# Block products by Strassen's scheme in the second feed-forward layer of a two-block transformer kernel

## Chip, cores and metric

One Trainium2 chip (trn2), one core. The metric is the device time of one execution in microseconds; three executions of the kernel before took 2068.88, 2069.16 and 2074.09 us, median 2069.16.

## What is computed

All in float32, 256 tokens, width 1024. A first transformer block (attention of two kinds, 32 experts with 4 chosen per token) is followed by two blocks: one with retention and one with an S5 state-space mixer, each with a gated, convolved feed-forward layer. The change concerns the feed-forward layer of the last block alone:

```python
def conv_ffn(h, w_up, conv_w, conv_b, w_down):
    val, gate = jnp.split(h @ w_up, 2, axis=-1)          # 1024 -> 2 x 2816
    gate = lax.conv_general_dilated(gate, conv_w, ..., padding=[(CONV_W - 1, 0)], ...) + conv_b   # 3 taps over tokens
    return (jax.nn.silu(gate) * val) @ w_down            # 2816 -> 1024

x = x + g2 * conv_ffn(h, ffn_w_up[i], ffn_conv_w[i], ffn_conv_b[i], ffn_w_down[i])
return rms_norm_2(x) * final_norm_g
```

## The kernel before

Activations lie transposed: a feature tile is 128 partitions, 256 tokens are the columns. Weights come through `ring`, six slots of 2 MB ("slabs"), filled by SP's queue in a fixed order; a slot is loaded again when the product that reads it has ended (`slab_left`). `plan()` (L221) numbers every PSUM chunk in the order in which PE makes them, and deals them to four banks in turn; `places()` (L353) deals the slabs to slots. Each engine's program is written out by hand. `begin` waits until a bank's last chunk was read, `end` signals `acc_ready`, readers wait for it with `read_ready` and give the bank back with `read_done`; `copied` waits for that signal. Four slots are held by the S5 mixer (`HELD`) and given back at slab `("glu", 2)`.

**Up.** 11 slabs of 8 k tiles x 512 features. `features` (L1058, matmul at L1074) makes 4 output tiles of 8 matmuls, each 128x128 weights on 256 columns; two output tiles make a chunk, a "pair". Pairs 0 to 10 are values: ACT copies them to `val` (`copy`, L1902). Pairs 11 to 21 are gates: ACT writes the tap of lag 0 and the bias (L2140), VectorE adds the lags 1 and 2 straight from PSUM (L2896, four operations), ACT takes tanh (L2157), and `finish` (L2918) makes the product with the value pair in two VectorE operations (L2923, L2926), one pair later.

**Down.** 8 slabs of 22 k tiles x 128 features; each is one chunk of 22 matmuls on 256 columns (L1074 again). Those of slab 0 wait pair by pair for `act_ready`. `add_to_x` (L2434) adds each to x, times the gate g2.

Ahead of up stands a norm: L2234 to L2263 on VectorE, then scale and shift of eight tiles on ACT (L1862), for each of which PE's first matmuls wait. Behind down stands the last norm: squares on ACT (L1808), sums on PE (L1096), L2232 to L2263 on VectorE, and the stores. GpSimd works for the S5 mixer (L3085 to L3204) and has nothing to do in this layer.

Other lines that are read below: L1394 and L1460 (gather and turning in the experts), L1745 and L1775 (S5 and glu products), L3018 (glu), L2837 and L2838 (retention, from PSUM), L3098 to L3109, L3185 and L3189 (GpSimd, for S5). GpSimd's L3098 to L3103 ran beside VectorE's `finish` of the first of the two feed-forward layers, which uses the same lines.

## Time and profile before

| | |
|---|---|
| median of three executions | 2069.16 us |
| span of the profiled execution | 2066.0 us (its time as a whole is not given; the median is 3.2 us above the span) |
| PE busy | 1958.7 us, 95% |
| VectorE busy | 632.7 us, 31% |
| ScalarE busy | 392.6 us, 19% |
| GpSimd busy | 201.1 us, 10% |
| second feed-forward layer, first up to last down matmul | 1827.11 to 2055.63 us |

Names in the rows: PE is TensorE's matmul, PEld its weight load, DVE is VectorE, ACT is ScalarE, POOL is GpSimd, SP the engine that issues the loads. Times are us from the start of the span, durations us unless marked ns. Each float32 matmul of the program stands as two records. "arena", "consts", "smalls", "ring" and "tiny" are SBUF tensors. Idle time of an engine that nobody waits for costs nothing.

### The profile page before, as it was taken

To read this page: it belongs to the slowest core of one execution; us is meant where nothing else is said; L and a number is where in the kernel's file an instruction comes from. 1 tells how busy PE (TensorE), PEld (TensorE's weight loads), DVE (VectorE), ACT (ScalarE), POOL (GpSimd) and SP (SyncE) were. 2 spreads that over 40 slices of the span, in tenths; PEclk is the share of its full clock that TensorE was granted. 3 is DMA by queue.
4 is the path that set the end of the run, shared out by engine and by line. 5 is a ranking of instruction groups with operands and counts; after the bars stand their busy time and mean duration, and the time that the engine had idled before them with its cause. 6 is when DMAs were issued, how large, how long until landed. Compare 5 with 4: busy or idle time off the path is not lost.

```text
span 2066.0 us, 24454 instructions
## 1 busy us (share of the span) xinstructions
PE 1958.7 (95%) x9820; PEld 1233.4 (60%) x9820; DVE 632.7 (31%) x1401; ACT 392.6 (19%) x759; POOL 201.1 (10%) x274
## 2 busy tenths in 40 slices
PE   7999999999898999989899999999999999999998
PEld 5645654433333443333334375788888889888887
DVE  3767342213212222112122255331004216210421
ACT  3125211110111111101111021220113215320211
POOL 0000000000000000000000000010745932200000
PEclk9999999999999999999999999999999999999999
DMA  9987799999999999999999996834343342634330
GB/s 373 367 306 247 272 378 407 427 425 426 429 428 429 429 428 429 428 429 428 429 428 428 414 365 221 319 112 145 121 163 123 140 166 95 237 135 146 112 112 21
DMA packets 120080, 615.40 MB, mean 298 GB/s; under 512 B 5344, under 2 KB 9568, under 8 KB 90560
## 3 DMA queue, kind: packets, MB, share of 16 engines
q1 hardware_dynamic: 118240, 604.43, 73.2%
q0 software_dynamic: 1760, 9.83, 1.3%
q8 instruction: 59, 0.97, 0.2%
q14 instruction: 21, 0.17, 0.0%
HBM read 613.20 MB, written 1.05 MB: 297 GB/s over the span
## 4 chain that ended last, share of the span: by engine, by line
PE 71%; DMA 20%; DVE 5%; ACT 2%; issue 1%; SPq 1%; POOL 1%; DVEq 0%; ACTq 0%; POOLq 0%
PE psum L1074 32%; PE psum L1439 20%; DMA ring<-in_w_in_dram 17%; PE psum L1085 3%; PE psum L1394 2%; PE psum L1405 2%; DMA arena<-in_cT_dram 2%; PE psum L1316 1%; PE psum L1589 1%; PE psum L1189 1%; DMA ring<-in_w_out_dram 1%; PE psum L1775 1%; PE psum L1121 1%; PE psum L1460 1%; PE psum L1217 1%
## 5 line engine op out<-in xcount | busy, mean ns | idle before, releaser
L1439 PE MATMUL psum<-ring,arena 128*64 128x512 f32 (+1 forms) x3200 | 687.4, 603 | 63.8 <-DMA ring<-in_w_in_dram 62.4
L1074 PE MATMUL psum<-arena,ring 128*128 128x256 f32 (+1 forms) x3072 | 680.4, 384 | 2.2 <-ACT arena L1862 1.4
L1074 PEld LDWEIGHTS psum<-arena,ring 128*128 128x128 f32 x3072 | 581.7, 190 | 99.0 <-issue 18.8
L1439 PEld LDWEIGHTS psum<-ring,arena 128*64 128x64 f32 (+1 forms) x3200 | 222.2, 135 | 502.7 <-issue 432.2
L1995 ACT ACTIVATE arena<-psum 128x512 f32<-128x512 f32 (+1 forms) x144 | 79.1, 571 | 730.5 <-PE psum L1439 724.9
L2575 DVE TENSOR_SCALAR arena<-consts,arena 128x64 f32<-128x64 f32 (+2 forms) x64 | 15.7, 309 | 317.3 <-PE psum L1439 317.3
L2896 DVE SCALAR_TENSOR_TENSOR consts<-psum,smalls,consts 128x255 f32<-128x255 f32 (+1 forms) x88 | 38.4, 478 | 229.9 <-ACT consts L2140 229.1
L2600 DVE TENSOR_TENSOR arena<-psum,arena 128x512 f32<-128x512 f32 x60 | 38.5, 683 | 221.6 <-PE psum L1460 221.6
L2557 DVE SCALAR_TENSOR_TENSOR x<-psum,mod,x 128x256 f32<-128x256 f32 x128 | 55.6, 479 | 136.0 <-PE psum L1405 135.9
L3068 POOL DMA_DIRECT2D arena<-in_pos_dram x1 | 0.5, 541 | 907.4 <-PE psum L1568 907.4
L1405 PE MATMUL psum<-arena 128*128 128x256 f32 (+1 forms) x272 | 68.1, 392 | 3.6 <-issue 1.5
L1902 ACT ACTIVATE arena<-psum 128x512 f32<-128x512 f32 (+1 forms) x49 | 27.3, 558 | 224.6 <-PE psum L1074 173.4
L1405 PEld LDWEIGHTS psum<-arena 128*128 128x128 f32 (+1 forms) x272 | 47.5, 189 | 30.8 <-issue 14.9
L2434 DVE SCALAR_TENSOR_TENSOR x<-psum,mod,x 128x256 f32<-128x256 f32 x28 | 13.0, 482 | 162.9 <-PE psum L1074 152.3
L1394 PE MATMUL psum<-arena 128*128 128x128 f32 x512 | 61.5, 280 | 0.0
L1394 PEld LDWEIGHTS psum<-arena 128*128 128x128 f32 x512 | 60.1, 196 | 0.0
L1085 PE MATMUL psum<-ring,arena 128*128 128x512 f32 x128 | 55.1, 592 | 0.0
L1808 ACT ACTIVATE sq<-x 128x512 f32<-128x512 f32 x24 | 15.0, 629 | 206.4 <-DVE x L2434 180.7
L2286 DVE SCALAR_TENSOR_TENSOR arena<-ring,cond,arena 128x512 f32<-128x512 f32 x70 | 52.6, 752 | 2.5
L2140 ACT ACTIVATE consts<-psum,smalls 128x256 f32<-128x256 f32 x44 | 22.5, 562 | 116.0 <-PE psum L1074 116.0
L1460 PE MATMUL psum<-consts,arena 128*128 128x128 f32 x256 | 37.8, 281 | 6.7 <-DVE arena L2600 5.6
L1460 PEld LDWEIGHTS psum<-consts,arena 128*128 128x128 f32 x256 | 27.1, 140 | 26.6 <-issue 19.3
(397 smaller groups left out, 1657.2 us busy)
## 6 DMA issues: line engine op xcount, KB each, us to landing
ring<-in_w_in_dram SPq DMA_DIRECT2D x120, 2048.0 KB, 17.1
ring<-in_w_out_dram SPq DMA_DIRECT2D x60, 2048.0 KB, 17.2
ring<-in_w_ada_dram SPq DMA_DIRECT2D x36, 2048.0 KB, 13.7
ring<-in_w_up_dram SPq DMA_DIRECT2D x22, 2048.0 KB, 7.9
ring<-in_w_ret_dram SPq DMA_DIRECT2D x12, 2048.0 KB, 16.4
ring<-in_w_down_dram SPq DMA_DIRECT2D x16, 1408.0 KB, 5.9
ring<-in_w_qkv_dram SPq DMA_DIRECT2D x4, 2048.0 KB, 20.1
ring<-in_w_in_dram SPq DMA_DIRECT2D x8, 1024.0 KB, 17.6
```

Source lines behind the costliest of these rows:

```text
L1074: ins = nc.tensor.matmul(bank(c)[:, at:at + n], w[:, k, m * P:m * P + P], r, start=(k == 0), stop=(k == k_tiles - 1))
L1085: ins = nc.tensor.matmul(bank((key, first_chunk + t))[:, 0:width], lhs(k, t), w[:, k, at:at + width], start=(k == 0), stop=(k == KD - 1))
L1394: ins = nc.tensor.matmul(psum[:, c, m * P:m * P + width], h_tok[:, t, k * P:k * P + P], sel[:, t, 0:width], start=(t == 0), stop=(t == TT ...
L1405: ins = nc.tensor.matmul(psum[:, 6 + c % 2, m * T:m * T + T], y[:, k * P:k * P + P], g, start=True, stop=True)
L1439: ins = nc.tensor.matmul(psum[at:at + size, p, :], act[:, k, n:n + size], w, start=(k < 3 - halves), stop=(k >= KD - 3 + halves))
L1460: ins = nc.tensor.transpose(out, of, con("ident"))
L1902: read_done(nc.scalar.activation(out, src, ACT.Copy, scale=scale), key)
L1995: nc.scalar.activation(out, src, ACT.Copy).then_inc(signal, 1)
L2286: ins = V.scalar_tensor_tensor(out=out, in0=w[:, k, :], scalar=c[:, k, :], in1=out, op0=ALU.mult, op1=ALU.add)
L2557: ins = V.scalar_tensor_tensor(out=x[:, k, :], in0=psum[:, 6 + c % 2, m * T:m * T + T], scalar=mod[:, 40 + k, 0:1], in1=x[:, k, :], op0=AL ...
L2600: ins = V.tensor_tensor(dst.rearrange("p k (e n) -> p k e n", n=CAP), src.rearrange("p k (e n) -> p k e n", n=CAP), bb.unsqueeze(3).to_bro ...
L2896: ins = V.scalar_tensor_tensor(out=cv[:, a, lag:T], in0=ps[:, a, 0:T - lag], scalar=w[:, 2 - lag, k:k + 1], in1=cv[:, a, lag:T], op0=ALU.m ...
```

## The change

The up product of layer 1 is cut per slab into a 2 x 2 block form: output features in two halves of 256 (i), k tiles in two halves of 4 (j), tokens in two halves of 128 (l). The down product is cut per two slabs: i is the slab, j the parity of the k tile, l the token half. Seven block products (Winograd's form) take the place of eight. PE makes them on 128 columns each: 7 x 8 matmuls per up unit, 7 x 11 per down unit.

- GpSimd makes S1 to S4 of the weights, four chained operations per unit, S1 in place of A21, the others in two sets of room taken from the arena and from two ring slots, so the ring has four slots in this layer. In down, S4 takes the room of S2, after product 6.
- VectorE makes T1 to T4 of the tokens: for up once, before it; for down four subtractions of 128x128 at the end of each pair.
- ACT copies product 1; VectorE adds up the others in seven operations per unit. Value and gate then both lie in SBUF, and the lagged sums read the gate from there. A pair is ready later: the blocks of i = 1 after products 5 and 4, those of i = 0 after products 2 and 3.
- The first down unit makes products 1, 6, 7, 5 jointly, pair by pair in the order in which the pairs become ready, then 2, 4, 3. Each down unit adds four 128x128 blocks to x; ACT's squares wait for `down_added`.
- The first up unit takes the order 1, 5, 6, 7, 2, 4, 3, and product 1 waits for four h tiles.

The core of the diff (of the functions, `seven_products` is PE's, the first `seven_up` ACT's, those from `with_sixth_product` on VectorE's, `weight_sums` and what follows it GpSimd's):

```diff
+PRODUCTS = {1: ("A11", "B11"), 2: ("A12", "B21"), 3: ("S4", "B22"), 4: ("A22", "T4"), 5: ("S1", "T1"),
+            6: ("S2", "T2"), 7: ("S3", "T3")}
+SEVEN = (1, 6, 7, 5, 2, 4, 3)
+SEVEN_FIRST = (1, 5, 6, 7, 2, 4, 3)
+SUM_NUMBER = {"S3": 1, "S1": 2, "S2": 3, "S4": 4}
+GATE_PAIRS = {layer: [0] + [m for s in range(6, 11) for m in (2 * s - 10, 2 * s - 11)] for layer in SEVEN_UP}
...
         if key == ("glu", 2):
-            queue = held + queue
+            queue = held[:2] + queue
...
+            def seven_products(key, a, b, blocks_ready=None, together=()):
...
+                def starts(p):
+                    begin((key, p))
+                    if PRODUCTS[p][0] in SUM_NUMBER:
+                        pe.wait_ge(weights_summed, 4 * unit + SUM_NUMBER[PRODUCTS[p][0]])
...
+                if together:
+                    for p in order[:4]:
+                        starts(p)
+                    for k in together:
+                        blocks_ready(k)
+                        for p in order[:4]:
+                            ins = part(p, k, 0, together[0], together[-1])
...
+                for p in order[4:] if together else order:
+                    starts(p)
+                    if blocks_ready and not together:
+                        blocks_ready(PRODUCTS[p][1])
+                    for m in range(m_tiles):
+                        for k in range(n_k):
+                            ins = part(p, k, m, 0, n_k - 1)
+                    end(ins)
...
+            def seven_up(layer):
+                done = 0
+                for s in range(11):
+                    late = range(done, done + pairs_of(s - 1))
+                    done += len(late)
+                    for n in late[:1]:
+                        if n:
+                            tanh(layer, n - 1)
+                        conv_begin(layer, n)
+                    copy_first(("up", layer, s), 2)
+                    for n in late[1:]:
+                        tanh(layer, n - 1)
+                        conv_begin(layer, n)
...
+            def with_sixth_product(key, m_tiles):
+                copied(dve, (key, 1))
+                read_done(plus_product(key, 6, m_tiles, first_product, with_sixth), (key, 6))
+                copied(dve, (key, 6))
+            def with_seventh_and_fifth(key, m_tiles, out):
+                read_done(plus_product(key, 7, m_tiles, with_sixth, with_seventh), (key, 7))
+                own.mark(plus_product(key, 5, m_tiles, with_sixth, with_fifth))
+                copied(dve, (key, 7))
+                read_done(plus_product(key, 5, m_tiles, with_seventh, out), (key, 5))
+                dve.wait_ge(dve_step, own.n)
+            def lagged_sums(layer, n):
...
+                for lag in (1, 2):
+                    for a in range(2):
+                        k = 2 * m + a
+                        own.mark(V.scalar_tensor_tensor(out=cv[:, a, lag:T], in0=gate[:, a, 0:T - lag],
+                                                        scalar=w[:, 2 - lag, k:k + 1], in1=cv[:, a, lag:T],
+                                                        op0=ALU.mult, op1=ALU.add))
+                    dve.wait_ge(dve_step, own.n)
+                V.memset(tiny[:, 499:500], 0.0).then_inc(conv_ready, 1)
+            def finish_pair(layer, n):
...
+                own.link(V.scalar_tensor_tensor(out=t, in0=t, scalar=1.0, in1=cv, op0=ALU.add, op1=ALU.mult))
...
+                V.scalar_tensor_tensor(out=v, in0=t, scalar=0.5, in1=v, op0=ALU.mult, op1=ALU.mult
+                                       ).then_inc(act_ready, 1)
+                dve.wait_ge(act_ready, 11 * layer + n + 1)
...
+                own.mark(sub("T3", "B22", "B12"))
+                own.link(sub("T1", "B12", "B11"))
+                own.link(sub("T2", "B22", "T1"))
+                sub("T4", "B21", "T2").then_inc(tokens_summed, 1)
+            def seven_up(layer):
+                first_sums(layer)
+                done = 0
+                for s in range(11):
+                    key = ("up", layer, s)
+                    late = range(done, done + pairs_of(s - 1))
+                    done += len(late)
+                    for n in late[:1]:
+                        lagged_sums(layer, n)
+                    with_sixth_product(key, 2)
+                    for n in late[:1]:
+                        if n:
+                            finish_pair(layer, n - 1)
+                    with_seventh_and_fifth(key, 2, up_out(s, 1, 1))
+                    for n in late[1:]:
+                        lagged_sums(layer, n)
+                    read_done(plus_product(key, 2, 2, first_product, up_out(s, 0, 0)), (key, 2))
+                    read_done(plus_product(key, 4, 2, with_seventh, up_out(s, 1, 0)), (key, 4))
+                    for n in late[1:]:
+                        finish_pair(layer, n - 1)
+                    read_done(plus_product(key, 3, 2, with_fifth, up_out(s, 0, 1)), (key, 3))
+                for n in range(done, 11):
+                    lagged_sums(layer, n)
+                    finish_pair(layer, n - 1)
+                finish_pair(layer, 10)
...
+            def weight_sums(key, a, free=None):
...
+                add("S3", "A11", "A21", ALU.subtract).then_inc(weights_summed, 1)
+                pool.wait_ge(weights_summed, n + 1)
+                add("S1", "A21", "A22", ALU.add).then_inc(weights_summed, 1)
+                pool.wait_ge(weights_summed, n + 2)
+                add("S2", "S1", "A11", ALU.subtract).then_inc(weights_summed, 1)
+                pool.wait_ge(weights_summed, n + 3)
+                if free:
+                    read_ready(pool, free)
+                add("S4", "A12", "S2", ALU.subtract).then_inc(weights_summed, 1)
...
+            read_ready(pool, ("s5y", S5_PARTS - 1))
+            for s in range(11):
+                in_place(("up", 1, s))
+                if s >= 2:
+                    read_ready(pool, (("up", 1, s - 2), 3))
+                weight_sums(("up", 1, s), up_weights(1, s))
+            for s in range(0, 8, 2):
+                for n in range(2):
+                    in_place(("down", 1, s + n))
+                read_ready(pool, (("down", 1, s - 4) if s >= 4 else ("up", 1, 8 + s // 2), 3))
+                weight_sums(("down", 1, s), down_weights(1, s), (("down", 1, s), 6))
```

`pairs_of(s)` is the number of gate pairs that up unit s makes: 0 to unit 4, one in unit 5, then two. `GATE_PAIRS` gives their order. So in unit s the engines work on the gate pairs of unit s - 1.

## Rows read from the trace of the kernel before

**Rows 1.** The page: VectorE's busy share, PE's and the granted clock in 40 slices.

```profile
PE 1958.7 (95%) x9820; PEld 1233.4 (60%) x9820; DVE 632.7 (31%) x1401; ACT 392.6 (19%) x759; POOL 201.1 (10%) x274
...
PEclk9999999999999999999999999999999999999999
```

**Rows 2.** Chain in order of time (start, us, what): the layer.

```profile
1827.11 228.53 PE psum L1074 x1056
```

**Rows 3.** Timeline (start, us, engine, line, xcount, idle before): gates of the layer.

```profile
1932.47 1.78 DVE L2896 SCALAR_TENSOR_TENSOR consts<-psum,smalls,consts 128x255 f32<-128x255 f32 x4 [3.57 <-ACT consts L2140]
...
1934.40 0.69 DVE L2923 SCALAR_TENSOR_TENSOR consts<-consts 128x512 f32<-128x512 f32 x1
1935.12 0.69 DVE L2926 SCALAR_TENSOR_TENSOR arena<-consts,arena 128x512 f32<-128x512 f32 x1
...
1938.25 1.02 ACT L2140 ACTIVATE consts<-psum,smalls 128x256 f32<-128x256 f32 x2 [5.37 <-PE psum L1074]
...
1939.38 1.79 DVE L2896 SCALAR_TENSOR_TENSOR consts<-psum,smalls,consts 128x255 f32<-128x255 f32 x4 [3.56 <-ACT consts L2140]
```

**Rows 4.** Timeline of VectorE in down: two of the eight additions to x.

```profile
1998.68 0.48 DVE L2434 SCALAR_TENSOR_TENSOR x<-psum,mod,x 128x256 f32<-128x256 f32 x1 [8.93 <-PE psum L1074]
2008.18 0.48 DVE L2434 SCALAR_TENSOR_TENSOR x<-psum,mod,x 128x256 f32<-128x256 f32 x1 [9.01 <-PE psum L1074]
```

**Rows 5.** Timeline of PE in the experts: matmuls on 128 columns.

```profile
263.44 5.45 PE L1394 MATMUL psum<-arena 128*128 128x128 f32 x32
...
303.11 1.09 PE L1460 MATMUL psum<-consts,arena 128*128 128x128 f32 x8
...
305.70 3.74 PE L1394 MATMUL psum<-arena 128*128 128x128 f32 x32
309.27 0.38 PE L1485 MATMUL psum<-consts,arena 128*128 128x128 f32 x2
```

**Rows 6.** Timeline of ACT and PE at the start of up.

```profile
1826.36 4.04 ACT L1862 ACTIVATE arena<-arena,mod,aff 128x256 f32<-128x256 f32 x8 [2.20 <-DVE arena L2263]
...
1827.11 3.07 PE L1074 MATMUL psum<-arena,ring 128*128 128x256 f32 x12 [0.45 <-ACT arena L1862]
```

**Rows 7.** Groups of GpSimd by form (busy us, mean ns): 512 and 1024 elements.

```profile
L3101 POOL TENSOR_TENSOR consts<-arena,tiny 128x512 f32<-128x512 f32 x4 | 4.2, 1057 | 0.0
...
L3185 POOL TENSOR_TENSOR consts<-tiny 128x1024 f32<-128x1024 f32 x1 | 1.9, 1912 | 0.1
```

**Rows 8.** DMA issues (KB each, median us to landing), 1780 to 2066.

```profile
ring<-in_w_down_dram SPq DMA_DIRECT2D x8, 1408.0 KB, 6.0
```

**Rows 9.** Timeline of VectorE: operations from PSUM on 256 and 128 columns, and one in glu.

```profile
1368.94 0.42 DVE L2837 TENSOR_TENSOR sq<-psum,consts 128x256 f32<-128x256 f32 x1
1369.28 0.28 DVE L2838 TENSOR_TENSOR sq<-psum,consts 128x128 f32<-128x128 f32 x1
...
1812.84 0.69 DVE L3018 SCALAR_TENSOR_TENSOR arena<-arena 128x512 f32<-128x512 f32 x1 [5.30 <-ACT arena L2214]
```

**Rows 10.** Timeline of VectorE and GpSimd where both run.

```profile
1588.52 1.78 DVE L2896 SCALAR_TENSOR_TENSOR consts<-psum,smalls,consts 128x255 f32<-128x255 f32 x4 [2.04 <-ACT consts L2140]
1588.49 1.09 POOL L3102 TENSOR_TENSOR arena<-arena,consts 128x512 f32<-128x512 f32 x1
...
1597.32 1.06 POOL L3098 TENSOR_TENSOR arena<-arena,tiny 128x512 f32<-128x512 f32 x1
1597.35 1.58 DVE L2923 SCALAR_TENSOR_TENSOR consts<-consts 128x512 f32<-128x512 f32 x1
1598.34 1.51 POOL L3099 TENSOR_TENSOR consts<-arena,tiny 128x512 f32<-128x512 f32 x1
1598.96 1.43 DVE L2926 SCALAR_TENSOR_TENSOR arena<-consts,arena 128x512 f32<-128x512 f32 x1
...
1693.56 1.88 POOL L3189 COPY sq<-tiny 128x2016 f32<-128x2016 f32 x1
1694.37 1.34 DVE L2234 TENSOR_TENSOR rstd<-rstd 128x256 f32<-128x256 f32 x1
```

**Rows 11.** Windows of PE (stretch, its length, busy, granted clock, DMA share, GB/s).

```profile
263.00:266.00 3.00, 3.00 (x20) 0.65 1.05 442
```

More of the change, by code:

```diff
@@ L221, in plan @@
 def plan():
-    chunks, slabs, bank, use = {}, {}, {}, {}
+    chunks, slabs, bank, use, units = {}, {}, {}, {}, {}
     uses = [0] * 6
@@ L243, in slab, with seven @@
         slabs[key] = len(chunks)
+    def seven(keys, order=SEVEN):
+        units[keys[0]] = len(units), order
+        chunk(*((keys[0], p) for p in order))
+        for key in keys:
+            slabs[key] = len(chunks)
     chunk(("norm", 1))
@@ L316, in ffn @@
         for s in range(11):
-            slab(("up", layer, s), 2)
+            if layer in SEVEN_UP:
+                seven([("up", layer, s)], SEVEN if s else SEVEN_FIRST)
+            else:
+                slab(("up", layer, s), 2)
             if layer == 0 and s == 0:
                 chunk(("cols", 8))
-        for s in range(8):
-            slab(("down", layer, s), 1)
+        for s in range(0, 8, 2):
+            if layer in SEVEN_DOWN:
+                seven([("down", layer, s), ("down", layer, s + 1)])
+            else:
+                slab(("down", layer, s), 1)
+                slab(("down", layer, s + 1), 1)
     ffn(0)
@@ L336, in plan @@
     chunk(("norm", 8))
-    return chunks, bank, use, slabs, rope_uses, before_loop
-CHUNK, BANK_OF, USE, SLABS, ROPE_USES, SLABS_1 = plan()
+    return chunks, bank, use, slabs, rope_uses, before_loop, units
+CHUNK, BANK_OF, USE, SLABS, ROPE_USES, SLABS_1, UNITS = plan()
 SLAB_KEYS = list(SLABS)
+UNIT_KEYS = list(UNITS)
 EARLY_SLABS = 1
@@ L812, in copied, with product, summed_tokens @@
             eng.wait_ge(acc_free[BANK_OF[key]], USE[key] + 1)
+        def product(key, p, m_tiles):
+            return psum[:, BANK_OF[(key, p)], 0:P * m_tiles]
+        def summed_tokens(kind, layer, n):
+            before = sum(4 * (at in SEVEN_UP) + 11 * (at in SEVEN_DOWN) for at in range(layer))
+            return before + n + (4 if kind == "down" else 0)
         def ln_of(guess):
@@ L874, in transformer_blocks_kernel @@
             7: [[(("glu", 2 + s // 2), s % 2)] for s in range(4)],
-            8: [[(("down", 1, 2 * s + a), 0) for a in range(2)] for s in range(4)],
         }
@@ L2118, in ffn @@
                 apply(5 + 2 * layer)
+                if layer in SEVEN_UP:
+                    seven_up(layer)
+                    for s in range(0, 8, 2):
+                        copy_first(("down", layer, s), 1)
+                    return
                 if layer == 0:
@@ new lines, in plus_product @@
+            def plus_product(key, p, m_tiles, a, out):
+                read_ready(dve, (key, p))
+                a, src = a[:, 0:P * m_tiles], product(key, p, m_tiles)
+                if len(out.shape) == 3:
+                    a, src = two(a), two(src)
+                else:
+                    out = out[:, 0:P * m_tiles]
+                return V.tensor_tensor(out, src, a, ALU.add)
+            def with_sixth_product(key, m_tiles):
+                copied(dve, (key, 1))
+                read_done(plus_product(key, 6, m_tiles, first_product, with_sixth), (key, 6))
+                copied(dve, (key, 6))
```

166 lines of the change are left out of this document (added).

## The prediction

> **What bounds the kernel now.** I read the page first: PE is busy nearly throughout at full granted clock and DVE under a third of the span [rows 1]. The chain in order of time then shows the second feed-forward layer as one piece, 228.53 us of L1074 with no other engine in it [rows 2]. So only matmul time counts there. One gate pair takes 6.91 us from L2896 to L2896 [rows 3], so an up slab (two pairs) takes 13.82 us; a down slab takes 9.50 us [rows 4]. The trace holds two records for each float32 matmul of the program: 1056 records are 11 x 32 + 8 x 22 = 528 matmuls, 0.433 us each, that is 0.216 us for half the columns. The span is 2066.0 us and the page gives no other time of that execution; the median of the runs is 3.2 us above the span. I add the change to the median.
>
> **Fewer columns: a gain.** A block product multiplies by 128 columns instead of 256. Per up unit 7 x 8 = 56 such matmuls stand for 32 full ones, per down unit (two slabs) 77 for 44. Their price: 32 records of L1394 run from 305.70 to 309.27 [rows 5], 0.1116 us each, so 0.223 us a matmul. Bounds: half a full one, 0.216, and the eight records of L1460, (1.09 - 0.28) / 7 = 0.116 us each, so 0.231 [rows 5]. I take 0.2235: same form, and the longest run. Up unit 12.52 us, 1.30 less, 11 times: -14.3. Down unit 17.21 against 19.0, 4 times: -7.2. **Clean gain 21.5 us.** A product takes 1.79 us in up, 2.46 in down. The two price bounds move about 700 matmuls (those that PE itself paces) by -5 to +5 us.
>
> **Start of up.** Before, PE starts at 1827.11, after the first h tile, and loses 0.5 us to tiles arriving each 0.49 us [rows 6]. Now product 1 waits for four tiles, 1.3 us later; T1 (0.69 us, one 128x512 operation, as L2923) and T2 fall under products 1 and 5. Net +0.8.
>
> **GpSimd's sums** are four chained TENSOR_TENSOR per unit of 1024 elements, 1.91 us each [rows 7], in down of 1408, 2.6 us by the slope from 512 to 1024. That is 7.7 us against a unit of 12.52 and 10.4 against 17.21, begun a whole unit ahead: hidden from PE. The ring has four slots instead of six; a down slab lands in 6.0 us [rows 8] and is asked for two units ahead: hidden. One place is short: S4 of the first down unit waits for product 6 and holds up the next unit's three sums: 10.7 us after product 6, wanted at about 10.4. +0.3. Up slabs 0 and 1 are now loaded when the first two glu slabs are done, and GpSimd's sums for them meet VectorE's glu operations, which sit idle 5.30 us ahead of each [rows 9]: hidden, and over before the norm. The queue of SP gets no new wait that PE notices.
>
> **VectorE's own work**, per gate unit. Seven reads of a product (0.42 us each, L2837 [rows 9]; back to back 0.36, chained 0.46): 2.8. Two lagged sums, 1.93 each from L2896 to L2923 [rows 3]: 3.86. Two finishes, 1.45 each, now with four subtractions of 128x128 (L2838 0.28 [rows 9], chained 0.32, together 1.14): 5.18. Sum 11.84 us in 12.52: just hidden. ACT, in its order tanh, conv_begin, copy of product 1, needs 4.1 us (1.02 for a pair [rows 3]) and its waits are met half a unit ahead. In the first six units VectorE has only the 2.8; in a down unit seven reads and four additions of 0.28 to 0.32, some 3.5 us in 17.2: hidden. Behind each read in VectorE's queue stand the lagged sums and finishes, and behind the reads stands PE, since four banks let it run at most four products ahead: a late VectorE stops PE within one unit.
>
> **The last pair.** After product 3 of unit 10 VectorE still owes the read, then lagged 9, finish 8, lagged 10, finish 9, finish 10: 1.93 + 2.59 + 1.93 + 2.59 + 2.59 = 11.6 us. PE covers 8.9 us with the ten earlier pairs of the joined products (40 matmuls). VectorE is 1.7 us late there, so even undisturbed PE waits 4.5 us. Before it waited for none.
>
> **The disturbance on which the sign hangs.** While GpSimd runs a TENSOR_TENSOR, VectorE operations with both inputs in SBUF wait for it: L2923 and L2926, 0.69 us alone, take 1.58 and 1.43 at 1597.35 while L3098 and L3099 run, and L3099 takes 1.51 instead of 1.06 [rows 10]. They take turns, and one GpSimd operation costs VectorE its length less 0.3 us. It holds for long ones: L2234 (0.42 alone) waits 0.92 us, until the 1.88 us L3189 has 0.15 us left [rows 10]. Operations that read PSUM are not held: the four L2896 at 1588.52 take 1.78 us, as without GpSimd [rows 3, 10]. In the change the lagged sums read the gate from SBUF, so they and the finishes and subtractions are all held; only the seven reads are free. Holding time per gate unit is 7.7 us of GpSimd plus some 8.5 us of VectorE, 16 us against 12.52. So I work out the chain, with 1.6 us for a held operation of 1024 and 2.3 for one of 1408. Time 0 is PE's end of unit 6, when the sums for unit 8 begin.
> Unit 7: read of product 3, 0.45; lagged sum held four times, 1.93 + 6.3 (8.7); read of 6 (9.1); finish (11.7); read of 7 at 12.1, which frees the bank for product 3, so PE ends unit 7 at 13.9, not 12.5. From there the sums for unit 9 hold a lagged operation 1.45, a finish 0.75 (0.8 goes under two reads), then 1.6 twice: 5.4. The read of 7 in unit 8 is at 12.1 + 11.84 + 5.4 = 29.3. In unit 9: again 5.4, and 7.0 by the first three sums of down, which GpSimd starts as soon as slab down 1 lands: 53.5. In unit 10 GpSimd waits: 65.4. Then 6.5 to the end of the unit's reads and 11.6 for the pairs: 83.5. Undisturbed PE would want the last pair at 4 x 12.52 + 8.9 = 59.0. **VectorE makes it 24.6 us late** (24 us of holding, of 15 operations and 30.7 us; 4.5 had come without it, but VectorE's slack of 0.7 a unit and its lateness are used up in it).
>
> The Trainium skill states the same coupling and speaks against this change: "SBUF — State Buffer", section "Who interferes with whom" and the list before it, calls the shared port pair an exclusive lock held for the whole instruction, against a VectorE operation with two SBUF inputs. The rows agree in kind and are 0.3 us short of the whole; by the whole length the sum would be some 4 us higher. The rest stands without it.
>
> **Clock.** With waits of up to 3.7 us in each gate unit and short bursts before the last pair, PE may resume at half clock: at 263 the granted clock is 0.65 and L1394 takes 5.45 us instead of 3.74 [rows 5, 11]. It matters once, after the last pair: +1.7 (0 to 3.4).
>
> **Tail.** Behind the last matmul one more 128x128 operation and two waits: +0.3.
>
> **Sum:** -21.5 + 0.8 + 0.3 + 24.6 + 1.7 + 0.3 = +6.2, so 2075.
>
> **Forecast and rivals.** A measurement of this kernel can tell 0.3%, 6.2 us, from no change.
> Forecast, 0.5: the gain is eaten in units 7 to 10, +6, slower by a hair. Its own range, with holding between 18 and 28 us: -1 to +12.
> Rival 1, 0.25, faster: the holding is mostly hidden, since GpSimd's operations fall on VectorE's reads and idle time (it has both in every unit, 2.8 and 0.7 us), or are shorter beside each other than here. It decides if less than about 10 of the 24 us is left. With none: -21.5 + 0.8 + 4.5 + 0.3 + 0.3 = -15.6, so 2054; half kept gives -8. For it: the steady unit fits without holding. Against: rows 10, where each meeting is paid.
> Rival 2, 0.15, clearly slower: PE falls to half clock in each gate unit, where a stall of 3.7 us precedes three products that the reads wait for; then the clock delays VectorE too. At 1.7 us in each of units 7 to 10 and twice after: 8.5 more in place of 1.7, +13; with each GpSimd operation paid whole +17, 2086. Against: the clock is 1.0 through the span's other waits [rows 1].
> Rival 3, 0.1: the half-width matmuls gain less, 0.231 us, and holding is as forecast: +5 more, 2080. That seven products stand for eight is certain from the counts.
>
> **Numbers.** 2075. Low: 2056, taking in most of rival 1; high 2086, rivals 2 and 3. The likeliest case's own range is 2068 to 2081. Faster by over 0.3%: 0.27 (rival 1 and a sliver). Within: 0.33 (the lower half of the forecast, part of rival 1). Slower: 0.40.
>
> **What would show it.** PE spacing 0.112 us a record in units 0 to 6, and 12.5 us a unit; DVE L2923 and the subtractions at 1.5 to 2.3 us instead of 0.69 and 0.28 in units 7 to 9, reads unchanged; PE waiting on DVE some 25 us between unit 7 and the first down product 2; POOL busy some 126 us more (11 x 7.7 + 4 x 10.4). The forecast is wrong if the lagged sums keep 0.48 us under a running GpSimd operation, or if the gate units last 12.5 us.

## The result, and the profile after the change

The kernel with the change is slower: 2088.8 us (median of 4 runs, 2086.78 to 2090.35) against 2071.6 us for the kernel before on the same chip (4 runs, 2068.88 to 2075.22). The ratio is 1.0087, 95% interval 1.0070 to 1.0103; the medians are 17 us apart. The forecast was 2075 in a range of 2056 to 2086: the side was right, the size was not, and the result lies outside the range.

The first part of the page after the change answers to [rows 1]:

```profile
PE 1954.6 (94%) x10612; PEld 1252.6 (60%) x10612; DVE 758.2 (36%) x1565; ACT 392.6 (19%) x763; POOL 357.7 (17%) x334
...
PEclk9999999999999999999999999999999999999899
```

PE is busy 4.1 us less in a span that is 22.5 us longer (2088.5 against 2066.0). DVE gained 125.5 us of busy time, though the change gives it far less arithmetic than that, and POOL gained 157, where 126 had been foreseen.

In the text below, "the layer" is the time from the first up matmul to the end of the last down matmul: 228.53 us before [rows 2]. After the change the chain of work in order of time reads (start, us, what; pieces in between are left out):

```profile
1831.12 75.29 PE psum L1179 x672
...
1906.86 4.82 DVE consts L3135 x2
...
1923.16 4.83 DVE consts L3135 x2
...
1967.99 5.55 DVE consts L3135 x2
1973.57 6.53 DVE consts L3135 x2
...
2013.58 6.32 POOL ring L3559 x2
...
2026.51 16.62 PE psum L1179 x132
2043.51 7.82 DMA ring<-in_w_down_dram
...
2062.91 14.99 PE psum L1179 x132
```

The layer now lasts from 1831.12 to 2077.90, **246.8 us**, 18.3 more. The one piece of [rows 2] has broken up. Units 0 to 5 are still PE's alone, 672 records in 75.29 us. From 1906, the first gate unit, the chain runs through VectorE's lagged sums, and in down through GpSimd's sums and a load. The other 4.2 us of the two spans: PE's first up matmul stands 2.22 us behind ACT's first h tile (0.75 in [rows 6]), the tail is 0.25 us longer, and 2.5 us came before the layer, where the code is the same; I leave those out.

VectorE's timeline after the change (start, us, engine, line, form, xcount). L3135 are the lagged sums, L3146, L3150 and L3158 a finish with its subtractions:

```profile
1923.08 9.87 DVE L3135 SCALAR_TENSOR_TENSOR consts<-ring,smalls,consts 128x255 f32<-128x255 f32 x4
...
1937.03 1.78 DVE L3135 SCALAR_TENSOR_TENSOR consts<-ring,smalls,consts 128x255 f32<-128x255 f32 x4
...
1939.52 2.09 DVE L3146 SCALAR_TENSOR_TENSOR consts<-consts 128x512 f32<-128x512 f32 x1
1941.65 2.72 DVE L3150 SCALAR_TENSOR_TENSOR arena<-consts,arena 128x512 f32<-128x512 f32 x1
1944.40 5.19 DVE L3158 TENSOR_TENSOR arena<-arena 128x128 f32<-128x128 f32 x4
...
1960.16 7.50 DVE L3158 TENSOR_TENSOR arena<-arena 128x128 f32<-128x128 f32 x4
...
1967.92 12.18 DVE L3135 SCALAR_TENSOR_TENSOR consts<-ring,smalls,consts 128x255 f32<-128x255 f32 x4
```

and GpSimd's beside it:

```profile
1922.85 2.36 POOL L3559 TENSOR_TENSOR arena<-ring 128x1024 f32<-128x1024 f32 x1 [6.49 <-PE psum L1179]
1925.29 2.41 POOL L3559 TENSOR_TENSOR ring<-ring 128x1024 f32<-128x1024 f32 x1
...
1938.71 10.41 POOL L3559 TENSOR_TENSOR ring<-ring 128x1024 f32<-128x1024 f32 x4 [6.04 <-PE psum L1179]
...
1969.90 9.92 POOL L3559 TENSOR_TENSOR ring<-ring 128x1408 f32<-128x1408 f32 x3
2013.55 12.81 POOL L3559 TENSOR_TENSOR ring<-ring 128x1408 f32<-128x1408 f32 x4 [33.73 <-PE psum L1179]
```

Four lagged sums take 1.78 us where GpSimd is idle (1937.03), as in [rows 3], and 9.87 us beside four of GpSimd's sums (1923.08): one VectorE operation for each of GpSimd's, held 2.02 us each. At 1967.92 GpSimd works on 1408 elements and the four take 12.18. The kind of holding is that of [rows 10]; the length is new: a sum of 1024 elements takes 2.40 us and one of 1408 3.18. The groups by form (busy us, mean ns) say the same, and that the reads of PSUM (L3109) are not held:

```profile
L3559 POOL TENSOR_TENSOR ring<-ring 128x1408 f32<-128x1408 f32 x16 | 50.9, 3184 | 48.2 <-PE psum L1179 45.8 <-issue 1.8
L3559 POOL TENSOR_TENSOR ring<-ring 128x1024 f32<-128x1024 f32 x21 | 50.4, 2398 | 16.0 <-PE psum L1179 14.6
...
L3109 DVE TENSOR_TENSOR consts<-psum,consts 128x256 f32<-128x256 f32 x33 | 13.5, 424 | 32.6 <-PE psum L1179 32.5
```

PE's timeline shows where it stood (the bracket is its wait):

```profile
1949.98 3.78 PE L1179 MATMUL psum<-sq,ring 128*128 128x128 f32 x16 [6.06 <-DVE ring L3109]
...
1980.70 3.78 PE L1179 MATMUL psum<-sq,ring 128*128 128x128 f32 x16 [7.18 <-DVE consts L3109]
...
2026.51 51.37 PE L1179 MATMUL psum<-arena,ring 128*128 128x128 f32 x440 [2.81 <-POOL ring L3559]
```

The two products behind the long waits take 3.78 us where 16 records otherwise take 1.79, at half clock (granted 0.50 from 1949.9 to 1953.5). The last line hides 2.2 us more: 440 records at 0.1117 are 49.2 us, not 51.37. Most of it is half clock too, behind the wait of 2.81 us. PE's windows (stretch, its length, PE busy, granted clock, DMA share, GB/s):

```profile
2026.50:2028.00 1.50, 1.49 (x11) 0.81 1.02 436
2028.00:2030.00 2.00, 2.00 (x11) 0.50 0.78 332
```

The first 132 of these records take 16.62 us (in the chain above), against 14.90 in a later version that does not wait there. So in down GpSimd's sums cost 2.8 us of waiting once, 1.7 of half clock behind it and some 0.5 over the rest, 5.0 in all.

### The profile page after: what moved, and what is told of

Read it like the earlier page. It is cut to its first block, busy times and chain, and to the rows that moved or that the text cites. A ratio compares the mean times of both kernels' runs of the same rounds, so it can differ in the third digit from the quotient of the medians.

```text
span 2088.5 us, 26401 instructions
## 1 busy us (share of the span) xinstructions
PE 1954.6 (94%) x10612; PEld 1252.6 (60%) x10612; DVE 758.2 (36%) x1565; ACT 392.6 (19%) x763; POOL 357.7 (17%) x334
## 3 DMA queue, kind: packets, MB, share of 16 engines
q8 instruction: 65, 1.06, 0.2%
## 4 chain that ended last, share of the span: by engine, by line
PE 66%; DMA 20%; DVE 8%; ACT 2%; POOL 2%; issue 2%; SPq 1%; DVEq 0%; ACTq 0%; POOLq 0%
PE psum L1160 21%; PE psum L1560 20%; DMA ring<-in_w_in_dram 18%; PE psum L1179 7%; PE psum L1206 3%; PE psum L1515 2%; DVE consts L3135 2%; PE psum L1526 2%; DMA ring<-in_w_qkv_dram 1%; PE psum L1437 1%; PE psum L1710 1%; PE psum L1310 1%; PE psum L1929 1%; POOL ring L3559 1%; PE psum L1242 1%
## 5 line engine op out<-in xcount | busy, mean ns | idle before, releaser
L1160 PE MATMUL psum<-arena,ring 128*128 128x256 f32 (+1 forms) x2016 | 453.6, 387 | 1.8 <-ACT arena L2018 0.9
L1160 PEld LDWEIGHTS psum<-arena,ring 128*128 128x128 f32 x2016 | 382.9, 191 | 70.6 <-issue 18.0
L2151 ACT ACTIVATE arena<-psum 128x512 f32<-128x512 f32 (+1 forms) x144 | 79.1, 571 | 730.2 <-PE psum L1560 724.6
L1179 PE MATMUL psum<-arena,ring 128*128 128x128 f32 x1048 | 126.9, 282 | 9.3 <-POOL ring L3559 2.8
L1179 PEld LDWEIGHTS psum<-arena,ring 128*128 128x128 f32 x1048 | 124.3, 199 | 10.7 <-issue 7.6
L3559 POOL TENSOR_TENSOR ring<-ring 128x1024 f32<-128x1024 f32 (+1 forms) x42 | 113.9, 2714 | 64.4 <-PE psum L1179 60.4
L2761 DVE SCALAR_TENSOR_TENSOR x<-psum,mod,x 128x256 f32<-128x256 f32 x128 | 55.6, 479 | 137.4 <-PE psum L1526 137.4
L1179 PE MATMUL psum<-sq,ring 128*128 128x128 f32 x512 | 66.3, 289 | 19.6 <-DVE consts L3109 11.0
L1179 PEld LDWEIGHTS psum<-sq,ring 128*128 128x128 f32 x512 | 63.5, 204 | 20.6 <-DVE consts L3109 11.6
L3239 DVE SCALAR_TENSOR_TENSOR consts<-psum,smalls,consts 128x255 f32<-128x255 f32 (+1 forms) x44 | 19.2, 478 | 108.8 <-ACT consts L2344 108.4
L2058 ACT ACTIVATE arena<-psum 128x512 f32<-128x512 f32 (+1 forms) x38 | 20.7, 547 | 158.8 <-PE psum L1160 106.0
```

The lines of the kernel that those rows point to most:

```text
L1160: ins = nc.tensor.matmul(bank(c)[:, at:at + n], w[:, k, m * P:m * P + P], r, start=(k == 0), stop=(k == k_tiles - 1))
L1179: return nc.tensor.matmul(product(key, p, m_tiles)[:, P * m:P * m + P], a[of_a][:, k, P * m:P * m + P], b[of_b][:, k, :], start=(k == firs ...
L2151: nc.scalar.activation(out, src, ACT.Copy).then_inc(signal, 1)
L2761: ins = V.scalar_tensor_tensor(out=x[:, k, :], in0=psum[:, 6 + c % 2, m * T:m * T + T], scalar=mod[:, 40 + k, 0:1], in1=x[:, k, :], op0=AL ...
L3559: return G.tensor_tensor(a[out], a[x0], a[x1], op)
```

## The experiments

**My theory** after the result: the clean gain is there, and it is lost to GpSimd's sums, by holding VectorE in units 6 to 10 and by coming late in down. **Rivals:** the half clock behind each wait is what delays the engines (rival 2 of the prediction); or VectorE's new work, the subtractions above all, is too much in itself. Single executions of the kernel before took from 2067.3 to 2080.5 us in all, on one chip alone up to 2079.0, so the whole time of one execution shows no difference of a few us; it is given beside the kernel before on the same chip, and the argument goes by the layer, read from each trace. (Of the one kernel that was traced twice, the layer is 221.6 us both times.) There is one execution each, unless rounds are named.

### No sums, and memsets in their place

```diff
-                    if PRODUCTS[p][0] in SUM_NUMBER:
-                        pe.wait_ge(weights_summed, 4 * unit + SUM_NUMBER[PRODUCTS[p][0]])
...
-                weight_sums(("up", 1, s), up_weights(1, s))
```

The first leaves all of GpSimd's sums out; PE multiplies by plain weight blocks in their place.

> Leaves out GpSimd's sums of the weights; PE takes blocks of the slabs in their place, and waits for no sum. Everything else of the change stays. Measured is the layer, from the first up to the last down matmul: 228.5 us before, 246.8 after. Holding theory (VectorE's operations on two SBUF inputs wait for GpSimd's): no holding, so only VectorE's own work is left, 924 matmuls of 0.2235 us and some 5 us before the last pair: 211 to 214 us. Rival, VectorE is overloaded by its own new operations whether or not GpSimd runs: 235 us or more, with VectorE's waits for PE near zero in units 7 to 10.

The second lets GpSimd write room of the same size for about as long, without reading:

```diff
-                    return G.tensor_tensor(a[out], a[x0], a[x1], op)
+                    own.link(G.memset(out, 0.0))
+                    own.link(G.memset(out, 0.0))
+                    return G.memset(out[:, 0:out.shape[1] // 2, :], 0.0)
```

> Puts two and a half memsets in place of each of GpSimd's sums, so that GpSimd is busy about as long at the same places and signals at about the same times, but reads nothing from SBUF. Leaves out the values of the sums. Rival, PE or VectorE wait because the sums come late: the layer stays at 240 to 247 us. Holding theory in the form in which the reading holds: VectorE's two-input operations keep 0.69 and 0.48 us, the layer takes 213 to 219 us. Holding theory in the form in which any GpSimd operation holds: about 245 us, with two-input operations of 1 to 2.5 us.

Measured: without sums the layer is **210.9 us** (1835.43 to 2046.30), with memsets **217.3** (1830.29 to 2047.55); whole 2058.79 and 2060.03 against 2068.22. Groups by form of the memset run, VectorE's lagged sums and GpSimd's first two memsets:

```profile
L3135 DVE SCALAR_TENSOR_TENSOR consts<-ring,smalls,consts 128x255 f32<-128x255 f32 x22 | 9.6, 479 | 0.1
...
L3560 POOL MEMSET ring<- 128x1024 f32 x21 | 20.1, 957 | 9.5 <-PE psum L1179 8.6
L3561 POOL MEMSET ring<- 128x1024 f32 x21 | 20.0, 952 | 1.2
```

GpSimd was as busy as with sums (0.96 + 0.95 + 0.53 us for one of 2.40), and VectorE's operations took 479 ns, as without GpSimd. So it is not GpSimd's work that holds VectorE but its reading of SBUF. The Trainium skill says this in "SBUF — State Buffer", section "Who interferes with whom": a VectorE instruction with two SBUF inputs contends with a GpSimd instruction that reads SBUF and not with one that only writes it. Both halves hold here.

The three layers split the loss. Memsets come as late in down as the sums do: their PE timeline has one wait for GpSimd of 3.21 us and 3.2 more within 440 records:

```profile
1995.23 52.32 PE L1179 MATMUL psum<-arena,ring 128*128 128x128 f32 x440 [3.21 <-POOL ring L3562]
```

That is the 217.3 - 210.9 = **6.4 us** of lateness, part of it again half clock (granted 0.50 from 1995.2 to 2000.5). The rest, 246.8 - 217.3 = **29.5 us**, comes with the reading: holding, and whatever half clock behind PE's longer waits adds to it. Four times the memsets take 13.2 us in down and four sums 12.8, so the memsets are the later ones: by the rows of the changed kernel itself lateness is 5.0 and holding 30.9.

### Sums of half the length

```diff
-                    return G.tensor_tensor(a[out], a[x0], a[x1], op)
+                    n = a[out].shape[1] // 2
+                    return G.tensor_tensor(a[out][:, 0:n, :], a[x0][:, 0:n, :], a[x1][:, 0:n, :], op)
```

Half of each sum is left out.

> Each of GpSimd's sums covers half of its elements (the other half is left out, and PE reads the summed half twice). The number of GpSimd operations and all waits stay; each takes about 1.25 us for 2.40 and 1.65 for 3.17. Holding theory with the whole length held less 0.35 us: 0.9 instead of 2.05 us a meeting, the layer at 218 to 226 us. Rival, the number of meetings counts and not their length (a fixed cost of taking turns): within 5 us of 246.8.

Measured: layer **219.1 us** (1834.08 to 2053.18), whole 2065.66 against 2068.22. Groups by form:

```profile
L3561 POOL TENSOR_TENSOR ring<-ring 128x512 f32<-128x512 f32 x21 | 28.0, 1335 | 30.0 <-PE psum L1180 28.6
L3561 POOL TENSOR_TENSOR ring<-ring 128x640 f32<-128x640 f32 x16 | 24.8, 1550 | 63.0 <-PE psum L1180 56.6 <-issue 5.8
```

With as many operations of about half the length, 8.2 us are left of the 35.9 between 210.9 and 246.8. Down has no wait for GpSimd here (its last 536 records take 60.14 us, without a gap), so the lateness is gone as a whole, and the 8.2 stand against the 29.5 to 30.9 of holding. The cost grows faster than the length. My reading is that short sums fall into VectorE's idle time and reads, and long ones don't fit there; no run separates that. This run also gives the price of a shorter sum from the ring: 1.33 us for 512, 2.40 for 1024, so 2.1 ns an element.

### PE kept busy in its waits

```diff
+                    keep_busy(FILL.get((key, p), 0))
                     starts(p)
```

33 extra matmuls stand in PE's program where it waits for VectorE.

> Nothing left out. PE makes matmuls into an unused bank where it waited for VectorE in the trace of after: 3 before product 4 of unit 6, 12 before product 5 of unit 8, 4 and 14 before products 5 and 4 of unit 9, each 0.43 us. Clock theory (after these waits PE ran 16 to 32 records at half speed, which lies on the chain): records of the products behind them at 0.112 us, layer shorter by 4 to 8 us, 239 to 243. Holding theory alone, where PE has slack there: within 2 us of 246.8.

Measured: layer **246.9 us** (1832.52 to 2079.43), whole 2091.89 against 2068.22. Several of the slow products ran at full clock (2.05 us for 16 records at 1920.27 and 1951.85, where 2.94 and 3.78 had stood), some did not (3.38 at 1934.95, 3.40 at 1973.52); the first products of up, at half clock in this run, cost 1.6 (76.92 us for 672 records instead of 75.29). Of the 8.8 us by which half clock lengthens PE's records in units 6 to 9 of the changed kernel, 3.0 are left here, and the layer, without the 1.6 at the start, is 1.5 us shorter. The run is not a clean price of the clock, though, since one filling was too long:

```profile
1978.54 6.21 PE L1270 MATMUL psum<-consts 128*128 128x256 f32 x28
```

It holds PE until 1984.6, and VectorE had given the bank back at 1981.3. What settles it is how long VectorE waits for PE in the changed kernel. Behind the two longest stretches at half clock it waits

```profile
1958.38 0.42 DVE L3109 TENSOR_TENSOR ring<-psum,consts 128x256 f32<-128x256 f32 x1 [0.41 <-PE psum L1179]
...
1998.03 0.42 DVE L3109 TENSOR_TENSOR ring<-psum,consts 128x256 f32<-128x256 f32 x1 [0.37 <-PE psum L1179]
```

and nowhere else from unit 7 to the last pair. In unit 6 it waits 1.58 and 2.10 us, and there full clock brought the second of these reads 1.6 us nearer to PE's start (3.9 us behind it here, 5.5 in the changed kernel). As long as the meetings stay where they are, the half clock therefore cost the gate units 2.4 us at most: elsewhere PE had to wait for VectorE anyway. Rival 2 falls as the main cause.

### No subtractions for down

```diff
-                own.mark(sub("T3", "B22", "B12"))
-                own.link(sub("T1", "B12", "B11"))
-                own.link(sub("T2", "B22", "T1"))
-                sub("T4", "B21", "T2").then_inc(tokens_summed, 1)
+                V.memset(tiny[:, 499:500], 0.0).then_inc(tokens_summed, 1)
```

The token sums of down are left out.

> Leaves out the four 128x128 subtractions at the end of each pair (T1 to T4 of the down product; PE takes blocks of val in their place). GpSimd is as in after. VectorE has 12 instead of 20 operations on two SBUF inputs per gate unit. Holding theory: the subtractions' own time before the last pair goes, 3 x 1.14 us, and about a third of the 29.5 us of holding (after less the run with memsets), but a GpSimd operation that met a subtraction may meet another operation instead: 228 to 237 us for the layer, against 246.8. Rival, holding depends on GpSimd's time alone: only the 3.4 us and VectorE's own 1.1 us a pair go where it is late, 240 or more.

Measured: layer **237.3 us** (1832.56 to 2069.9), just above the 228 to 237 expected, whole 2082.37 against 2080.48. The lagged sums are held more than before, 1107 and 1158 ns on average against 1058 and 1106, and L3150 takes 1319 against 877 (groups by form): what GpSimd would have held in the subtractions it holds in other operations. VectorE has 12.6 us less of its own work (11 x 1.15) and the layer gets 9.5 us shorter, still 26 above the layer without sums. VectorE's work is a part of the cost only because it is stretched.

### One product alone

Up in seven products, down as before:

```diff
-SEVEN_DOWN = (1,)
+SEVEN_DOWN = ()
```

> Only the up product in seven products; down as before (eight slabs, 22 matmuls of 256 columns, slab 0 in the order in which the pairs become ready), no sums and no subtractions for down. Nothing left out. Holding theory: 137.7 us of matmuls in up, 76.0 in down, 0.8 at the start, some 13 us of holding left over VectorE's slack of 3 us a unit, 1 to 3 us before the last pair: 227 to 232 us for the layer, about as before (228.5). Rival, up is where the gain is and down spoils it (its sums and subtractions): 216 to 222.

Down in seven products, up as before:

```diff
+N_SEVEN = 0
...
-            if layer in SEVEN_UP:
+            if layer in SEVEN_UP and s < N_SEVEN:
```

> Only the down product in seven products; up as before (the gates are read from PSUM), with the four subtractions per pair and GpSimd's sums for down as in after. Nothing left out. Holding theory: up 152.5 us; VectorE's reads from PSUM are not held and it has 2 us of slack a pair, so holding costs at most 2 us; down 68.8 us and the 6.4 us by which its sums are late: 227 to 231. Rival, holding in the gate units costs as much here too: 235 or more.

Measured: up alone **228.95 us** (1834.62 to 2063.57), whole 2075.78 against 2080.48; down alone **232.3 us** (1834.43 to 2066.70), whole 2079.16 against 2080.48; the latter is a little above the 227 to 231 expected. Up alone gains 14.3 by its matmuls; it gives 12.5 back in its gate units and 2.6 at the last pairs in down slab 0. Down alone gains 7.2 and loses 11; its PE timeline:

```profile
1990.20 22.67 PE L1179 MATMUL psum<-arena,ring 128*128 128x128 f32 x176 [3.23 <-DVE consts L3199]
2015.70 51.00 PE L1179 MATMUL psum<-arena,ring 128*128 128x128 f32 x440 [2.83 <-POOL ring L3537]
```

The joined products need four free banks at once and so wait 3.23 us until VectorE has read the last pair; behind that wait PE is at half clock (granted 0.50 from 1990 to 1995), and the 176 records take 22.67 us where 19.7 would do; GpSimd's late sums cost 2.83, and the half clock behind them (0.50 from 2017 to 2019) 1.8 more. Together the two parts lose 18.3, apart +0.4 and +3.8: the other 14 us come from their meeting. My reading is that the subtractions of down lengthen VectorE's share of the gate units and that GpSimd's sums for down fall into the same units; how the 14 us divide between the two was not tried.

### Seven products where no pair is open

With the same condition, five units and no down:

```diff
-SEVEN_DOWN = (1,)
+SEVEN_DOWN = ()
+N_SEVEN = 5
```

> Seven products in the five up slabs that make only values; the other six slabs of up, and down, as before. Nothing left out. VectorE has only the seven reads from PSUM while GpSimd adds. Holding theory: 5 x 1.30 us less and 0.8 more at the start, 222 to 224 us for the layer. Rival, GpSimd's sums disturb PE or the loads too: 226 or more.

The layer took 221.6 us (1833.49 to 2055.1), a little less than the 222 to 224 expected, whole 2067.35 against 2080.48. Then timed, in 5 rounds:

> The kernel with seven products in the five value-only up slabs and everything behind them as before, timed. Its one look had the layer at 221.6 us against 228.5 before, a gain of 6.9 (5 x 1.30 = 6.5 by the price of the half-width matmul, and no meeting of GpSimd's sums with VectorE's lagged sums or finishes). Theory (the half-width matmuls pay, GpSimd's sums beside the pairs lose): 2062 to 2065 against 2069 to 2072, ratio 0.996 to 0.998. Rival (the gain of one look was the chip's spread): a ratio whose interval holds 1.

Measured: **2064.95 us** against 2070.39, ratio 0.997 (0.9958 to 0.9983); layer 221.6 again (1832.73 to 2054.37). PE's timeline after the last product of unit 4 is one piece, 736 records from 1895.33 in 159.02 us, as before the change. 228.5 - 5 x 1.30 - 0.5 (the h tiles of [rows 6]) is 221.5.

The same with down in seven products too, and with room of its own for S4:

```diff
-                    "A22": w[1][:, 1:KF:2, :], "S1": w[1][:, 0:KF:2, :], "S2": s2, "S3": s3, "S4": s2}
+                    "A22": w[1][:, 1:KF:2, :], "S1": w[1][:, 0:KF:2, :], "S2": s2, "S3": s3, "S4": s4}
```

> Seven products in up slabs 0 to 4 and in all four down units, the gate slabs as before; S4 of a down unit has room of its own, so GpSimd's sums never wait for product 6. Theory: 221.6 (values alone) - 7.2 (four down units of 17.2 instead of 19.0) + about 3 for the last pair, whose four products PE makes jointly and for which VectorE must finish and subtract while GpSimd works on the second down unit, + 1 to 2 for additions to x held by the sums = 218 to 220 for the layer, 2060 to 2063 as a whole. GpSimd's sums for the first two down units are made in the gate slabs beside VectorE, whose own work there is 4.8 us in 13.8, so holding fits there. Rival (holding counts wherever GpSimd works beside VectorE, slack or not): six operations of 2.9 us of holding in the gate slabs reach PE through the joined products, 222 to 230.

Measured: **2072.40 us** against 2070.39, ratio 1.0004 (0.9991 to 1.0016); layer **228.7** (1833.07 to 2061.7). The theory's 218 to 220 was wrong by 9 us, and the rival's 222 to 230 holds it. VectorE's and PE's timelines and PE's windows (stretch, its length, PE busy, granted clock, DMA share, GB/s) where up ends:

```profile
1985.54 3.53 DVE L3241 SCALAR_TENSOR_TENSOR arena<-consts,arena 128x512 f32<-128x512 f32 x1
1989.11 9.73 DVE L3249 TENSOR_TENSOR arena<-arena 128x128 f32<-128x128 f32 x4
```
```profile
1982.52 12.01 PE L1180 MATMUL psum<-arena,ring 128*128 128x128 f32 x80 [3.79 <-DVE consts L3200]
1998.89 7.59 PE L1180 MATMUL psum<-arena,ring 128*128 128x128 f32 x52 [4.37 <-DVE arena L3249]
```
```profile
1982.50:1987.00 4.50, 4.48 (x21) 0.50 0.33 136
...
1998.90:2002.00 3.10, 3.10 (x14) 0.50 0.00 0
```

With room of its own GpSimd began the second unit's sums at 1985.33, just where VectorE was finishing the last pair: L3241 and the subtractions of that finish took 13.3 us instead of 1.84 (0.69 + 1.15). I had given the last pair 3 us; PE's two waits for it are 8.2. The first sums, from 1956.91 in the gate slabs, had held three operations by 7.9 us in all, and yet counted from the end of unit 4 VectorE begins its last finish only 0.6 us later than in the version below that makes no sums there: holding did fit in the gate slabs, so the rival's range holds the result but its reason does not. Half clock takes 21 and 14 records 4.48 and 3.10 us where 2.35 and 1.57 would do. The first 2.1 us only shorten the wait of 4.37 that follows; the 1.5 behind that wait lie on the chain. With a wait of 0.93 us for a late sum these parts (8.2, 2.1, 1.5, 0.9) are 12.8 of the 14.4 us by which the layer is longer than its matmuls ask for (228.5 - 0.5 - 6.5 - 7.2 = 214.3).

### Seven products, with the last pairs left alone

The remedy: down slabs 0 and 1 as before (they cover the last pairs, as in the kernel before), seven products in slabs 2 to 7, and GpSimd starts its sums for down when the last pair is done.

```diff
         for s in range(0, 8, 2):
-            if layer in SEVEN_DOWN:
+            if layer in SEVEN_DOWN and s:
...
+            pool.wait_ge(tokens_summed, 15)
+            for s in range(2, 8, 2):
```

> Seven products in up slabs 0 to 4 and in the last three down units (slabs 2 to 7); gate slabs and down slabs 0 and 1 as before, and GpSimd makes no sum of down weights until VectorE has finished the last pair. Theory (the half-width matmuls give 1.30 a unit in up and 1.79 in down, holding costs nothing where no pair is open, joined products behind a late VectorE were the cost of the version with four down units): 228.5 - 5 x 1.30 - 3 x 1.79 = 216.6, + up to 1 for the start and for x additions = 216.6 to 218 for the layer, 2057 to 2060 against some 2070, ratio 0.994 to 0.996, faster than both kernels. Rival (down in seven products loses what it gains also without joined products, by slabs or sums that come late): 219 to 222, ratio 0.997 or more. PE should show no wait on VectorE, and its waits for GpSimd or DMA in the last three units tell how late the sums are.

The other run is the same without that wait:

> As the version before, but GpSimd makes the sums for slabs 2 and 3 as soon as these have landed, by the slots about 7 us before the end of up, beside VectorE's work on pairs 8 to 10. Theory (four operations of 1408 elements hold VectorE 2.9 us each, 8 to 12 us in all, of which some 5 are covered by its idle time and PE wants the last pair only 8.6 us after up's end): 1 to 5 us more than that version. Rival (sums beside VectorE cost nothing where PE needs its results late): within 0.5 us of it.

Measured, 5 rounds: **2059.42 us** against 2071.01, ratio **0.9939** (0.9926 to 0.9953), and 2063.89 for the run without the wait, ratio 0.996 (0.9946 to 0.9974). Chain in order of time of the first of the two, whole layer:

```profile
1829.81 64.40 PE psum L1180 x560
1894.21 101.88 PE psum L1161 x472
1996.08 51.60 PE psum L1180 x462
```

Layer **217.9 us** (1829.81 to 2047.7), one unbroken chain of PE again. By the prices: 228.5 - 0.5 - 6.5 - 5.4 = 216.1, and the first 560 records took 64.40 us instead of 62.77, 1.6 more, at a granted clock of 0.66 in the stretch from 1829 to 1834 (64.40 us in the other run too). GpSimd's sums still hold VectorE in down, where nobody waits for it:

```profile
1985.29 9.63 POOL L3540 TENSOR_TENSOR ring<-ring 128x1408 f32<-128x1408 f32 x3 [106.31 <-DVE arena L3251]
```
```profile
2008.95 3.00 DVE L3161 SCALAR_TENSOR_TENSOR x<-consts,mod,x 128x128 f32<-128x128 f32 x1
...
2015.43 0.35 DVE L3161 SCALAR_TENSOR_TENSOR x<-consts,mod,x 128x128 f32<-128x128 f32 x1
```

An addition to x takes 3.00 us beside a sum and 0.35 alone, seven of the twelve are met, and PE has no wait. Without the wait, GpSimd started at 1982.79 instead of 1985.29, 2.5 us earlier, and met the finish of the last pair:

```profile
1983.18 3.53 DVE L3243 SCALAR_TENSOR_TENSOR arena<-consts,arena 128x512 f32<-128x512 f32 x1
```

PE then waits 1.20 us for L3243 in down slab 0, and the layer is 219.4 (1829.64 to 2048.99), 1.5 more, at the lower end of the 1 to 5 expected (the slabs land later than I had reckoned, so only the last finish is met). The two ratios' intervals overlap, so the 4.5 us between the medians are not shown by this pair; the 1.5 us in the layer stand in the traces.

## Why the prediction was right or wrong

The layer lost 18.3 us, the start 1.5 and the tail 0.25: +20.0 in the two profiled executions, against +6.2. By the prediction's steps:

- **Clean gain, -21.5: right.** 672 records in 75.29 us are 0.112 each, 0.224 us a matmul, against 0.2235 taken; rival 3 (0.231) falls. The layer without sums, 210.9, is 924 x 0.2235 = 206.5 and 4.4 us of waits at the last pairs.
- **Start, +0.8: right.** 1.47 us more ahead of the first matmul, 0.5 saved behind it: +1.0.
- **Sums late in down, +0.3: wrong.** 6.4 by the difference of two runs, 5.0 by the rows of the changed kernel itself, of which 1.7 are half clock behind the wait. The step said "10.7 us after product 6, wanted at about 10.4". At 3.18 us each, four sums take 12.8, and the wait is 2.8. The rest, some 0.5, is a part that I had called hidden: the last slab lands too late for its sums (the 7.82 us of load in the chain).
- **The last pair without holding, 4.5 us: right** (4.4).
- **Holding, 24.6 with that: wrong in size.** It measured 29.5 + 4.4 = 33.9, or 30.9 + 4.4 = 35.3 by the rows. The failed step is "with 1.6 us for a held operation of 1024 and 2.3 for one of 1408". I took a sum's length from L3185, 1.91 us [rows 7], the only row with 1024 elements on all partitions; the sums of the weights take 2.40 and 3.18, and a held operation waits 2.02 and about 2.85 longer (the latter from L3249 above, 9.73 for 1.15 with three meetings). In my chain this gives, for the holding of units 7 to 9, 8.1 + 7.5 + 16.8 = 32.4 us (the timeline's 9.87, 2.09, 2.72, 5.19, 7.50 and 12.18 less their lengths alone) instead of 6.3 + 5.4 + 5.4 + 7.0 = 24.1. The same 0.4 us four times over also made the first gate unit late, unit 6, which I had left out because with 1.6 it just fitted: PE waits 1.90 us there. 24.6 + 8.3 + 1.9 = 34.8, reckoned after the result. In PE's rows it shows as 24.0 us of waits for VectorE (25 were foreseen) and 8.8 of slow records. The same lengths explain GpSimd's busy time: 44 x 2.40 + 16 x 3.18 = 156.5 us, where 126 was foreseen.
- **Clock, +1.7, once, after the last pair: right in size, at another place.** The joined products, where I had placed it, ran at full clock (the last 96 records in 11.01 us); the 1.7 stand behind the wait for the sums in down, on the chain. Half clock in the gate units came too, as rival 2 had said (8.8 us in PE's records), but it delayed VectorE by 2.4 us at most, and these are part of the 33.9.
- **Tail, +0.3: right.**

Sum of what was measured: -21.5 + 1.0 + 6.4 + 33.9 + 0.25 = +20.0, with the clock in the 6.4 and the 33.9. The mechanism of the forecast is the one that decided, and rival 1 (holding mostly hidden) falls; the range was too narrow on this side because it varied how many meetings there would be and not how long each is. Dearer rows were there to be read in the trace of before: L3077 adds two whole halves of 512 elements in 1.26 to 1.63 us, beside the 1.06 of L3101 that [rows 7] show. But L3102, whose two operands are whole as well, takes 1.09. So the rows did spread from 1.06 to 1.36 on average, I used the low end alone, and whole operands by themselves are not what makes a sum long. The Trainium skill, too, has the dearer price: "GPSIMD Engine Reference", section "Elementwise — side-by-side cycle accounting", gives 4497 ns for an addition of 2048 float32 elements, an estimate of 2.25 us for 1024 by that page and 3.1 for 1408. The runs agree within 7% (2.40 and 3.18); I had not used it.

What stays open: why a sum of 512 elements from the ring takes 1.33 us where L3102 takes 1.09 in the kernel before, and one of 1024 2.40 where L3185 takes 1.91; and whether seven products in the gate slabs would pay with the sums made by another engine or at another time, which was not tried.

## What to carry to other kernels

Work given to GpSimd is not free because PE does not wait for it: here each sum that met a VectorE operation with two SBUF inputs stopped it for nearly its whole length (2.02 us of 2.40), so count the meetings and price them by the dearest row of the same operation as well as by the cheapest. A saving in PE's work is worth having only in stages where the engines behind it have slack for the added work and its holding; here five slabs of eleven and six of eight were such stages, and the cut version is 0.6% faster than the kernel it came from while the full one is 0.9% slower. Delaying the helper until the critical engine is done took one wait instruction and made the layer 1.5 us shorter (217.9 against 219.4).

## What was not expected of the hardware

- A memset on GpSimd does not hold VectorE at all: 479 ns a lagged sum beside 0.95 us memsets, as without any GpSimd work, against 1058 beside sums.
- GpSimd's price per element is not one number: 128x1024 float32 took it 2.40 us in the sums and 1.91 at L3185, 128x512 1.33 in the halved sums, 1.27 at L3077 (median) and 1.09 at L3102. Both operands are whole in all of these but L3185; what makes the difference is not shown.
- Half clock behind a wait shows in PE's rows (3.78 us for 16 records instead of 1.79) and may be worth almost nothing, as in the gate units (2.4 us at most of 8.8), or its whole length, as behind the wait for the sums in down (1.7 us) and behind the last pair of the version with down in seven products (1.5 us). It depends on who is next on the path.
